# Moving one channel tile of a depthwise convolution from VectorE to GpSimd, and fewer taps at both ends of the GLU projection

## Chip, cores and metric

One NeuronCore of a Trainium2 chip runs the whole kernel. The metric is device time in microseconds, the median of several executions. TensorE does matmuls and transposes, VectorE (DVE in the rows), ScalarE (ACT) and GpSimd (POOL) do elementwise work, and SyncE (SP) issues most of the DMAs.

## What is computed

One layer of a decoder for a prompt of 1024 tokens and 8 sequences of 4 new tokens (1056 tokens together, float32):

```python
z = rms_norm(x) @ w_in        # q, k, v | GLU value, GLU gate | gate a, gate b
u = ua * sigmoid(ub)                            # (T, 1024)
c = conv(u_ext, width 31, one filter per channel) + b   # causal, depthwise
A = three-group dilated window attention @ w_att
B = silu(layer_norm(c)) @ w_conv_out
x = x + (sigmoid(ga) * A + sigmoid(gb) * B) @ w_out
x = x + swiglu(rms_norm(x))
```

The outputs also hold the updated key/value windows and the last 30 rows of `u`. The depthwise convolution of one channel is a sum of 31 products: output token t takes `w[tau] * u[t + tau]` for tau from 0 to 30, from `u` with 30 rows of history ahead of it.

## The kernel before

Activations lie with channels on the 128 partitions: 1024 channels are 8 tiles (`KT`), each 1056 tokens long, handled by TensorE in three chunks of 352 (`NCH`). Every product in full precision is split into three matmuls (lines 678 to 680), from a high and a low part of both operands. A weight job is one 1024×128 slice of a weight: SyncE loads it into `raw`, ScalarE casts the high part `whi` (line 1140 or 1203), VectorE subtracts to make the low part `wlo` (`split_lo`, line 1428), and TensorE runs 72 matmuls. `raw`, `whi` and `wlo` have two buffers each; the weights of job m + 2 are made when job m is over.

The jobs come in this order, written out by hand on each engine: 16 GLU jobs (0 to 15, two for each channel tile j of `u`), 18 jobs for Q, K and V (16 to 33, three groups of six), 16 jobs for the gates, 8 for the convolution's projection, then attention projection, `w_out` and the FFN. From the gate jobs on, engines walk through 72 slots `q`, one chunk of 352 tokens each. Attention blocks, moves of V and K rows (`moves`, slots 1, 13 and 29 and the ones after), LayerNorm (from slot 22) and the samples' attention are hung on those slots.

The convolution runs on VectorE beside all this. `tap(k, tau)` (lines 1466 to 1472) adds one product for 1024 tokens of channel tile k: the first tap of a tile is a `tensor_scalar`, the other 30 are `scalar_tensor_tensor` with `u` and `conv` as the two tensors. 8 × 31 = 248 taps are spread by fixed counts: 13 after each GLU tile, 5 in each Q/K/V job (split 1, 2, 2 over its chunks, between the evacuations `qkv_out`), and 3 in each slot for the 54 that are left. `sample_conv(k)` (lines 1498 to 1508) does the 32 sample tokens of a tile by a product, a reduction and a bias. It runs for tiles 0 to 5 in every third Q/K/V job, ahead of that job's `split_lo`, and for tiles 6 and 7 behind the last tap of each, in slots 7 and 17.

VectorE's `qkv_out` (lines 1512 to 1527) moves a finished Q/K/V chunk out of PSUM and signals `s_zfd`, for which TensorE's job after next waits; for q and k it needs ScalarE's root of the mean square (`rsb`).

In a gate slot VectorE does, in this order: `split_lo` where it is due, `probs_in`, `maxima`, moves, then the slot's taps. `maxima` is followed by ScalarE's exponentials (`pb`, line 1246) and TensorE's transposes of them (`turn_probs`, line 879).

GpSimd issues DMAs only: 16 cache copies from HBM to HBM at fixed points (`cache_copy`, line 625; each waits for a certain `wlo`), then the cache tiles for the samples' attention, which wait for the end of LayerNorm, and more cache copies.

Of the kernel before, what the change touches and what calls it, by code (L numbers as in the profile page):

```python
# [17 lines left out]
F32 = mybir.dt.float32  # L18
F32R = mybir.dt.float32r
ALU = mybir.AluOpType  # L20
# [4 lines left out]
P = 128  # L25
D = 1024
SEQ = 1024
DEC_B, DEC_S = 8, 4
NS = DEC_B * DEC_S
T = SEQ + NS  # L30
NCH = 3
CH = T // NCH
PC2 = SEQ - 2 * CH
KT = D // P
HD = 64
NG, NH = 3, 4
# [4 lines left out]
CW = 31  # L41
HIST = CW - 1
SEG = HIST + DEC_S
ULEN = HIST + SEQ + DEC_B * SEG
# [15 lines left out]
QKV0 = GLU0 + 2 * KT  # L60
# [23 lines left out]
KTILES = [1] * 10 + [1, 2, 1, 2, 1, 2, 1] + [0] + [1] * 4  # L84
KTILE_SLOT = 31

TAPS_GLU = 13
TAPS_QKV = 5
TAPS_SLOT = 3
V_B, V_LW, V_LB, V_NF = CW, CW + 1, CW + 2, CW + 3  # L90
NVEC = CW + 4
# [3 lines left out]
def build(nc, a):  # L95
# [4 lines left out]
    def at(name, shape, dt, offset):  # L100
        return nc.alloc_sbuf_tensor_at(name, shape, dt, offset=offset)
# [16 lines left out]
    vec = perm("vec", [P, KT, NVEC])  # L118
# [14 lines left out]
    conv = at("conv", [P, KT, T], F32, S3)  # L133
# [5 lines left out]
    U0 = misc + 5 * T * 4  # L139
    u = at("u", [P, KT, ULEN], F32, U0)  # L140
# [46 lines left out]
    pb = reg("pb", [P, NH, 2 * P])  # L187
    kvv = reg("kvv", [P, KT, GW])
    assert cur2[0] <= nc.sbuf_usable_end
    rowqk = at("rowqk", [P, NG, 2, HD], F32, U0 + KT * ULEN * 4 + 3 * GW * 4)  # L190
    cur2 = [cur2[0] - KT * GW * 4]
    prow = reg("prow", [P, NG, 2 * P])
# [37 lines left out]
    def sem(name):  # L230
        return ctx.enter_context(nc.semaphore(name))
# [7 lines left out]
    s_hi, s_lo, s_pe = sem("s_hi"), sem("s_lo"), sem("s_pe")  # L239
    s_z = [sem(f"s_z{i}") for i in range(2)]  # L240
    s_zfd = [sem(f"s_zfd{i}") for i in range(2)]
    s_g, s_gfd, s_a, s_af = (sem(n) for n in ("s_g", "s_gfd", "s_a", "s_af"))
    s_ufree = sem("s_ufree")
    s_sig = sem("s_sig")
    s_sq, s_ssr, s_msr, s_sqrt = sem("s_sq"), sem("s_ssr"), sem("s_msr"), sem("s_sqrt")
    s_ztd, s_zta = sem("s_ztd"), sem("s_zta")
    s_zst = [sem(f"s_zst{i}") for i in range(2)]
# [86 lines left out]

        return ob[n % 4] if n < 2 * KT else ob2[(n - 2 * KT) % 3]

    TAP0 = KT * TAPS_GLU + 6 * NG * TAPS_QKV

    UNITS = [("att", c * KT + j) for c in range(2) for j in range(KT)] + [("out", 0), ("out", 1)]
    UNITS += [("att", 2 * KT + j) for j in range(KT)] + [("out", o) for o in range(2, DNG)]  # L340
# [275 lines left out]
    @block.gpsimd  # L616
    def _(pool):
        caches = ("cache_kv_w128", "cache_kv_w512", "cache_kv_w2048")

        def cache_copy(g, b, q=0, parts=1):  # L620
            keep = WIN[g] - DEC_S
            src = a[caches[g]][0, b, DEC_S:WIN[g]].rearrange("t k h d -> t (k h d)")
            dst = a[f"kv_sample{g}"][0, b, 0:keep].rearrange("t k h d -> t (k h d)")
            r = slice(q * keep // parts, (q + 1) * keep // parts)
            pool.dma_start(dst[r, :], src[r, :]).then_inc(s_cache, 16)

        for b in range(DEC_B):
            pool.wait_ge(s_lo, 2 * b + 3)
            cache_copy(0, b)
        for b in range(DEC_B):  # L630
            pool.wait_ge(s_lo, 4 * b + 3)
            cache_copy(1, b)

        def cache_tile(n, kind, g, b):

            c = a[caches[g]][0, b, :, kind].rearrange("t h d -> t (h d)")
            if n >= 3 and n - 3 < NB:

                pool.wait_ge(s_sc, n - 3 + 1)
            elif n >= 3:  # L640

                pool.wait_ge(s_kcf, n - 3 - NB + 1)
            if g == 0:
                pool.dma_start(kc[n % 3][:, DEC_S - 1, :], c).then_inc(s_kc[n % 3], 16)
            else:
                pool.dma_start(kc[n % 3][:, :, :], c.rearrange("(i r) d -> i r d", r=DIL[g])[:, 0:DEC_S, :]).then_inc(s_kc[n % 3], 16)

        pool.wait_ge(s_ln["norm"], NCH)
        for n in range(NB):
            g, b = n // DEC_B, n % DEC_B  # L650
            cache_tile(n, 0, g, b)
            if b == 0:
                pool.wait_ge(s_srows, 16 * (g + 1))
            if n >= 2:

                pool.wait_ge(s_prod, n - 1)
            pool.dma_start(qb[n % 2][:, :, :].rearrange("p s d -> p (s d)"),
                           scr_q[g, 0, DEC_S * b:DEC_S * b + DEC_S, :].rearrange("r d -> (r d)").partition_broadcast(P)).then_inc(s_qb[n % 2], 16)
        for n in range(NB):
            cache_tile(NB + n, 1, n // DEC_B, n % DEC_B)  # L660

        for b in range(DEC_B):
            for q in range(4):
                pool.wait_ge(s_lo, FFN0 + 1 + (4 * b + q) * 2)
                cache_copy(2, b, q, 4)
        pool.dma_start(a["conv_sample"][0, :, 0:HIST - DEC_S, :], a["state_conv"][0, :, DEC_S:HIST, :]).then_inc(s_cache, 16)
# [6 lines left out]
    def _(pe):  # L673
# [163 lines left out]
        def moves(g, part):  # L837
            if part == 0:
                if g == 0:
                    pe.wait_ge(s_urow, 2)  # L840
                    pe.wait_ge(s_zfd[1], NCH * GATE0 // 2)
                elif g == 1:
                    pe.wait_ge(s_Oe, KT)
                else:
                    pe.wait_ge(s_ln["cen"], NCH)
                    pe.wait_ge(s_ln["root"], NCH)
            for i in (range(5) if part == 0 else range(5, NMOVE[g])):
                move(g, i)
# [574 lines left out]
    def _(dve):  # L1423
# [51 lines left out]
        for j in range(KT):  # L1475
            split_lo(0, 2 * j + 2, j + 1)
            for c in range(NCH):
                dve.wait_ge(s_sig, NCH * j + c + 1)
                dve.wait_ge(s_z[0], NCH * j + c + 1)
                n = CH if c < 2 else PC2  # L1480
                last = V.tensor_tensor(u[:, j, HIST + c * CH:HIST + c * CH + n], z(0, c)[:, 0:n], sg[:, c * CH:c * CH + n], ALU.mult)
                if c == 2:
                    last = V.tensor_tensor(u[:, j, HIST + SEQ:].rearrange("p (b r) -> p b r", b=DEC_B)[:, :, HIST:SEG],
                                           z(0, c)[:, n:CH].rearrange("p (b s) -> p b s", b=DEC_B),
                                           sg[:, SEQ:T].rearrange("p (b s) -> p b s", b=DEC_B), ALU.mult)

                last.then_inc(s_zfd[0], 1)
                dve.drain().then_inc(s_zfd[1], 1)
            split_lo(1, 2 * j + 3, j + 1)
            if j == 0:  # L1490
                conv_params()
            for v in range(TAPS_GLU * j, TAPS_GLU * (j + 1)):
                tap(v // CW, v % CW)
        V.tensor_copy(ptail[:, :, :], u[:, :, SEQ:SEQ + HIST])
        V.tensor_copy(utail[:, :, :].rearrange("p k (b s) -> p k b s", b=DEC_B),
# [2 lines left out]
        def sample_conv(j):  # L1498
            us = u[:, j, HIST + SEQ:].rearrange("p (b r) -> p b r", b=DEC_B)
            win = bass.AP(us.tensor, us.offset, [us.ap[0], [SEG, DEC_B], [1, DEC_S], [1, CW]])  # L1500
            wv = vec[:, j, 0:CW]
            wr = bass.AP(wv.tensor, wv.offset, [wv.ap[0], [0, DEC_B], [0, DEC_S], [1, CW]])
            dve.drain()
            V.tensor_tensor(sprod[:, :, :, :], win, wr, ALU.mult)
            dve.drain()
            V.tensor_reduce(conv[:, j, SEQ:T], sprod[:, :, :, :].rearrange("p b s w -> p (b s) w"), AX_X, ALU.add)
            dve.drain()
            return V.tensor_scalar(conv[:, j, SEQ:T], conv[:, j, SEQ:T], vec[:, j, V_B:V_B + 1], None, ALU.add)
# [21 lines left out]
        for g in range(NG):  # L1530
            for i in range(6):
                m = QKV0 + 6 * g + i
                for c in range(NCH):
                    if m > QKV0:
                        qkv_out(m - 1, c)
                    v0 = KT * TAPS_GLU + TAPS_QKV * (m - QKV0)
                    for v in range(v0 + (0, 1, 3)[c], v0 + (1, 3, 5)[c]):
                        tap(v // CW, v % CW)
                if (m - QKV0) % NCH == 0:
                    last = sample_conv((m - QKV0) // NCH)  # L1540
                    if (m - QKV0) // NCH == 4:
                        last.then_inc(s_ufree, 1)
                split_lo(m % 2, m + 2, m // 2 + 1)
# [37 lines left out]
        def ln_sum(c):  # L1581

            if c == 0:
                dve.drain()
            if c == 2:
                dve.wait_ge(s_ln["mean"], 1)
            acc = csum[:, c % 2, :, :]
            V.tensor_tensor(acc, conv[:, 0:2, cols(c)], conv[:, 2:4, cols(c)], ALU.add)
            for k in range(4, KT, 2):
                dve.drain()  # L1590
                V.tensor_tensor(acc, acc, conv[:, k:k + 2, cols(c)], ALU.add)
            dve.drain()
            V.tensor_tensor(acc[:, 0, :], acc[:, 0, :], acc[:, 1, :], ALU.add).then_inc(s_ln["sum"], 1)
# [108 lines left out]
        for q in range(NSLOT):  # L1702
# [11 lines left out]
            for g in range(NG):  # L1714
# [3 lines left out]
                if q == MOVE_SLOT[g] + 1:  # L1718
                    for i in range(5, NMOVE[g], 2):
                        move_rows[0](dve, g, i, s_kvd)  # L1720
            for v in range(TAP0 + TAPS_SLOT * q, min(TAP0 + TAPS_SLOT * (q + 1), KT * CW)):
                tap(v // CW, v % CW)
                if v == (KT - 1) * CW - 1:
                    sample_conv(KT - 2)
                if v == KT * CW - 1:
                    sample_conv(KT - 1)
                    dve.drain()
            if q == MEAN_SLOT - 1:
                ln_sum(0)
                ln_sum(1)  # L1730
# [202 lines left out]
```

## Time and profile before

| | |
|---|---|
| Median of 3 executions | 1866.09 us (1861.48 to 1867.97) |
| The profiled execution | 1861.45 us |
| Its span, first to last instruction | 1859.7 us |
| TensorE, VectorE, ScalarE, GpSimd busy | 95%, 56%, 34%, 4% of the span |
| Mean granted clock of TensorE | 0.968 of full speed |

In a timeline or chain, a row gives start and duration in us, engine and line, and the result and inputs by name. A bracket holds the idle time of the engine just ahead of it and what ended it. `DVEq` is VectorE's instruction queue (drains, semaphores), `PEld` is the weight load.

### The profile page before, as it was taken

The page shows a single profiled execution, that of the slowest core. Times are in us where ns is not written, and L with a number is a line of the kernel's source. Part 1 is how long each engine was busy: PE and PEld are TensorE (multiplying, and loading weights), DVE is VectorE, ACT ScalarE, POOL GpSimd, SP SyncE. Part 2 cuts the span into 40 slices and gives each one's busy share as a digit, 9 for nine tenths or more (in the row PEclk, how much of TensorE's full clock was granted, in tenths as well). Part 3 has the DMA queues.
Part 4 walks back from the last instruction along what each step waited for, and adds up shares of the span by engine and source line. Part 5 has one row for each costly group of instructions (what it writes and reads, how often), then busy time and mean ns, then how long its engine had stood idle before and what let it go on. Part 6 is the DMA issues. An engine that isn't in the chain of part 4 may idle for free.

```text
span 1859.7 us, 25335 instructions
## 1 busy us (share of the span) xinstructions
PE 1764.4 (95%) x10357; PEld 1656.8 (89%) x10357; DVE 1046.0 (56%) x1464; ACT 623.6 (34%) x1029; POOL 69.8 (4%) x125
## 2 busy tenths in 40 slices
PE   6999989999999887689999999999999999999999
PEld 5899989999888877679998889899899899899897
DVE  5688888788887665663275432424424424424425
ACT  5111165957566676710122322111111111111110
POOL 0000000000000011212000000000000000000000
PEclk8999999999999998888799999999999999999999
DMA  6111333234342436965382012222222222222232
GB/s 191 57 56 56 102 112 115 92 114 139 102 141 87 143 114 201 341 220 174 103 277 91 1 37 96 93 90 87 91 93 87 93 90 87 94 90 88 93 109 103
DMA packets 156487, 211.55 MB, mean 114 GB/s; under 512 B 9090, under 2 KB 127010, under 8 KB 155603
## 3 DMA queue, kind: packets, MB, share of 16 engines
q1 hardware_dynamic: 145971, 134.01, 23.4%
q0 software_dynamic: 10416, 76.16, 10.8%
q8 instruction: 68, 1.11, 0.2%
q14 instruction: 32, 0.26, 0.0%
HBM read 180.04 MB, written 74.80 MB: 137 GB/s over the span
## 4 chain that ended last, share of the span: by engine, by line
PE 83%; DVE 7%; DMA 4%; DVEq 2%; SPq 2%; ACT 1%; issue 1%; ACTq 0%
PE ps L678 19%; PE ps L679 19%; PE ps L680 19%; PE ps L1116 4%; PE ps L1114 4%; PE ps L1115 4%; DVE conv L1472 2%; PE ps L945 2%; PE ps L1044 2%; PE ps L1046 2%; PE ps L1045 2%; DMA qb<-scr_q 2%; DMA raw<-w_in 1%; PE ps L892 1%; SPq L474 1%
## 5 line engine op out<-in xcount | busy, mean ns | idle before, releaser
L678 PE MATMUL ps<-xhi,whi 128*128 128x352 f32 x1200 | 406.5, 339 | 8.6 <-DVEq L1527 7.0
L680 PE MATMUL ps<-xhi,wlo 128*128 128x352 f32 x1200 | 389.1, 324 | 0.0
L679 PE MATMUL ps<-xlo,whi 128*128 128x352 f32 x1200 | 388.6, 324 | 0.0
L678 PE MATMUL ps<-nhi,whi 128*128 128x352 f32 x1056 | 341.7, 324 | 0.0
L679 PE MATMUL ps<-nlo,whi 128*128 128x352 f32 x1056 | 339.4, 321 | 0.0
L680 PE MATMUL ps<-nhi,wlo 128*128 128x352 f32 x1056 | 339.0, 321 | 0.0
L1472 DVE SCALAR_TENSOR_TENSOR conv<-u,vec,conv 128x1024 f32<-128x1024 f32 x240 | 308.3, 1284 | 25.6 <-issue 11.1
L1428 DVE TENSOR_TENSOR wlo<-raw,whi 128x1024 fp32r<-128x1024 f32 x126 | 153.5, 1220 | 254.7 <-ACT whi L1203 246.5
L678 PEld LDWEIGHTS ps<-xhi,whi 128*128 128x128 f32 x1200 | 228.9, 191 | 19.6 <-DVEq L1527 7.6
L679 PEld LDWEIGHTS ps<-xlo,whi 128*128 128x128 f32 x1200 | 229.2, 191 | 4.4 <-issue 0.2
L680 PEld LDWEIGHTS ps<-xhi,wlo 128*128 128x128 f32 x1200 | 228.4, 190 | 0.0
L678 PEld LDWEIGHTS ps<-nhi,whi 128*128 128x128 f32 x1056 | 198.9, 188 | 1.1
L679 PEld LDWEIGHTS ps<-nlo,whi 128*128 128x128 f32 x1056 | 199.1, 189 | 0.4
L680 PEld LDWEIGHTS ps<-nhi,wlo 128*128 128x128 f32 x1056 | 198.6, 188 | 0.0
L1203 ACT CAST whi<-raw 128x1024 fp32r<-128x1024 f32 x90 | 93.9, 1045 | 279.0 <-PE ps L1109 209.2
L1867 DVE TENSOR_TENSOR x<-x,ps 128x512 f32<-128x512 f32 x176 | 118.2, 686 | 78.8 <-PE ps L1116 78.4
L1116 PE MATMUL ps<-whi,aclo 128*128 128x512 f32 x352 | 138.8, 394 | 0.0
L1114 PE MATMUL ps<-whi,achi 128*128 128x512 f32 x352 | 138.8, 394 | 0.0
L1115 PE MATMUL ps<-wlo,achi 128*128 128x512 f32 x352 | 138.2, 393 | 0.0
L1854 DVE TENSOR_TENSOR sil<-ps,sil 128x352 f32<-128x352 f32 x66 | 34.6, 525 | 124.4 <-PE ps L680 124.4
L1404 ACT ACTIVATE sil<-ps 128x352 f32<-128x352 f32 x66 | 30.7, 465 | 190.4 <-PE ps L680 190.4
L678 PE MATMUL ps<-shi,whi 128*128 128x352 f32 x192 | 69.0, 360 | 25.3 <-DVE slo L1696 24.5
(214 smaller groups left out, 2242.8 us busy)
## 6 DMA issues: line engine op xcount, KB each, us to landing
kv_sample<-cache_kv_w POOLq DMA_DIRECT2D x32, 1022.0 KB, 6.4
raw<-w_in SPq DMA_DIRECT2D x50, 512.0 KB, 4.6
raw<-w_gate_up SPq DMA_DIRECT2D x44, 512.0 KB, 3.9
scr_z<-zt SPq DMA_DIRECT2D x34, 528.0 KB, 3.2
kc<-cache_kv_w POOLq DMA_DIRECT2D x32, 512.0 KB, 6.1
qb<-scr_q POOLq DMA_DIRECT2D x24, 512.0 KB, 6.5
raw<-w_down SPq DMA_DIRECT2D x22, 512.0 KB, 4.2
kv_sample<-cache_kv_w POOLq DMA_DIRECT2D x8, 1016.0 KB, 6.5
```

Source lines behind the costliest of these rows:

```text
L678: pe_mm(out, wh, rhs_hi, start=first, stop=False)
L679: pe_mm(out, wh, rhs_lo, start=False, stop=False)
L680: return pe_mm(out, wl, rhs_hi, start=False, stop=last)
L945: mm = nc.tensor.matmul(ps[:, 3, hp * P + col:hp * P + col + w], kc[m % 3][:, s if g else DEC_S - 1, hp * P:(hp + 1) * P], ptr[:, g, 0, co ...
L1044: nc.tensor.matmul(dst, hhi[:, k, tok], wohi[half][:, k, :], start=k == 0, stop=False)
L1114: nc.tensor.matmul(dst, achi[i % 2][:, k, tok], whi[half][:, cc], start=k == 0, stop=False)
L1115: nc.tensor.matmul(dst, achi[i % 2][:, k, tok], wlo[half][:, cc], start=False, stop=False)
L1116: mm = nc.tensor.matmul(dst, aclo[i % 2][:, k, tok], whi[half][:, cc], start=False, stop=k == 1)
L1203: act.copy(whi[n % 2][:, :], raw[n % 2][:, :]).then_inc(s_hi, 1)
L1428: V.tensor_tensor(wlo[slot][:, :], raw[slot][:, :], whi[slot][:, :].bitcast(F32), ALU.subtract).then_inc(s_lo, 1)
L1472: return V.scalar_tensor_tensor(dst, src, w, dst, ALU.mult, ALU.add)
L1867: last = V.tensor_tensor(x1_half(t, half), x1_half(t, half), ps[0:n, d % RING, :], ALU.add)
```

## The change

The 31 taps of channel tile 7 go to GpSimd. It starts when the last GLU tile of `u` is there (`s_zfd[0]`), multiplies each shifted row into one of two new buffers `ctap`, drains, and adds that to `conv`: one `tensor_scalar` for tap 0, then 30 times a `tensor_scalar` and a `tensor_tensor`. It signals `s_conv` behind the last. Four of the 1016 KB cache copies now stand ahead of this on GpSimd's queue and four behind it. `ctap` lies over the start of buffers that the attention stage uses, so TensorE waits for `s_conv` before the first `moves`, and VectorE waits for it before the first sum of LayerNorm.

VectorE keeps 217 taps. It runs 6 after the first GLU tile and 8 after the last (13 before), 3 in the first Q/K/V job (5 before), and three in each of slots 0 to 12. The sample convolutions of tiles 6 and 7 stand in slots 2 and 4.

```diff
--- before.py
+++ after.py
@@ -84,8 +84,9 @@
 KTILES = [1] * 10 + [1, 2, 1, 2, 1, 2, 1] + [0] + [1] * 4
 KTILE_SLOT = 31
 
-TAPS_GLU = 13
-TAPS_QKV = 5
+TAPS_GLU = (6, 13, 13, 13, 13, 13, 13, 8)
+TAPS_QKV = (3, 5)
+KT_DVE = KT - 1
 TAPS_SLOT = 3
 V_B, V_LW, V_LB, V_NF = CW, CW + 1, CW + 2, CW + 3
 NVEC = CW + 4
@@ -187,6 +188,7 @@
     pb = reg("pb", [P, NH, 2 * P])
     kvv = reg("kvv", [P, KT, GW])
     assert cur2[0] <= nc.sbuf_usable_end
+    ctap = [at(f"ctap{i}", [P, SEQ], F32, U0 + KT * ULEN * 4 + 2048 + i * SEQ * 4) for i in range(2)]
     rowqk = at("rowqk", [P, NG, 2, HD], F32, U0 + KT * ULEN * 4 + 3 * GW * 4)
     cur2 = [cur2[0] - KT * GW * 4]
     prow = reg("prow", [P, NG, 2 * P])
@@ -241,7 +243,7 @@
     s_zfd = [sem(f"s_zfd{i}") for i in range(2)]
     s_g, s_gfd, s_a, s_af = (sem(n) for n in ("s_g", "s_gfd", "s_a", "s_af"))
     s_ufree = sem("s_ufree")
-    s_sig = sem("s_sig")
+    s_sig, s_conv = sem("s_sig"), sem("s_conv")
     s_sq, s_ssr, s_msr, s_sqrt = sem("s_sq"), sem("s_ssr"), sem("s_msr"), sem("s_sqrt")
     s_ztd, s_zta = sem("s_ztd"), sem("s_zta")
     s_zst = [sem(f"s_zst{i}") for i in range(2)]
@@ -334,7 +336,7 @@
 
         return ob[n % 4] if n < 2 * KT else ob2[(n - 2 * KT) % 3]
 
-    TAP0 = KT * TAPS_GLU + 6 * NG * TAPS_QKV
+    TAPQ = [sum(TAPS_GLU) + (TAPS_QKV[0] + (n - 1) * TAPS_QKV[1] if n else 0) for n in range(6 * NG + 1)]
 
     UNITS = [("att", c * KT + j) for c in range(2) for j in range(KT)] + [("out", 0), ("out", 1)]
     UNITS += [("att", 2 * KT + j) for j in range(KT)] + [("out", o) for o in range(2, DNG)]
@@ -627,7 +629,22 @@
         for b in range(DEC_B):
             pool.wait_ge(s_lo, 2 * b + 3)
             cache_copy(0, b)
-        for b in range(DEC_B):
+        for b in range(4):
+            pool.wait_ge(s_lo, 4 * b + 3)
+            cache_copy(1, b)
+
+        pool.wait_ge(s_zfd[0], NCH * KT)
+        for tau in range(CW):
+            k = KT - 1
+            dst, src, w = conv[:, k, 0:SEQ], u[:, k, tau:tau + SEQ], vec[:, k, tau:tau + 1]
+            if tau == 0:
+                last = nc.gpsimd.tensor_scalar(dst, src, w, vec[:, k, V_B:V_B + 1], ALU.mult, ALU.add)
+            else:
+                nc.gpsimd.tensor_scalar(ctap[tau % 2][:, :], src, w, None, ALU.mult)
+                pool.drain()
+                last = nc.gpsimd.tensor_tensor(dst, dst, ctap[tau % 2][:, :], ALU.add)
+        last.then_inc(s_conv, 1)
+        for b in range(4, DEC_B):
             pool.wait_ge(s_lo, 4 * b + 3)
             cache_copy(1, b)
 
@@ -837,6 +854,7 @@
         def moves(g, part):
             if part == 0:
                 if g == 0:
+                    pe.wait_ge(s_conv, 1)
                     pe.wait_ge(s_urow, 2)
                     pe.wait_ge(s_zfd[1], NCH * GATE0 // 2)
                 elif g == 1:
@@ -1489,7 +1507,7 @@
             split_lo(1, 2 * j + 3, j + 1)
             if j == 0:
                 conv_params()
-            for v in range(TAPS_GLU * j, TAPS_GLU * (j + 1)):
+            for v in range(sum(TAPS_GLU[:j]), sum(TAPS_GLU[:j + 1])):
                 tap(v // CW, v % CW)
         V.tensor_copy(ptail[:, :, :], u[:, :, SEQ:SEQ + HIST])
         V.tensor_copy(utail[:, :, :].rearrange("p k (b s) -> p k b s", b=DEC_B),
@@ -1533,8 +1551,8 @@
                 for c in range(NCH):
                     if m > QKV0:
                         qkv_out(m - 1, c)
-                    v0 = KT * TAPS_GLU + TAPS_QKV * (m - QKV0)
-                    for v in range(v0 + (0, 1, 3)[c], v0 + (1, 3, 5)[c]):
+                    v0, n = TAPQ[m - QKV0], TAPQ[m - QKV0 + 1] - TAPQ[m - QKV0]
+                    for v in range(v0 + n * c // NCH, v0 + n * (c + 1) // NCH):
                         tap(v // CW, v % CW)
                 if (m - QKV0) % NCH == 0:
                     last = sample_conv((m - QKV0) // NCH)
@@ -1581,6 +1599,7 @@
         def ln_sum(c):
 
             if c == 0:
+                dve.wait_ge(s_conv, 1)
                 dve.drain()
             if c == 2:
                 dve.wait_ge(s_ln["mean"], 1)
@@ -1718,13 +1737,12 @@
                 if q == MOVE_SLOT[g] + 1:
                     for i in range(5, NMOVE[g], 2):
                         move_rows[0](dve, g, i, s_kvd)
-            for v in range(TAP0 + TAPS_SLOT * q, min(TAP0 + TAPS_SLOT * (q + 1), KT * CW)):
+            for v in range(TAPQ[-1] + TAPS_SLOT * q, min(TAPQ[-1] + TAPS_SLOT * (q + 1), KT_DVE * CW)):
                 tap(v // CW, v % CW)
-                if v == (KT - 1) * CW - 1:
-                    sample_conv(KT - 2)
-                if v == KT * CW - 1:
-                    sample_conv(KT - 1)
-                    dve.drain()
+            if q in (2, 4):
+                sample_conv(KT - 2 + (q - 2) // 2)
+            if q == 4:
+                dve.drain()
             if q == MEAN_SLOT - 1:
                 ln_sum(0)
                 ln_sum(1)
```

## Rows read from the trace of the kernel before

**Rows 1.** The page: busy time by engine, and TensorE and VectorE in 40 slices.

```profile
PE 1764.4 (95%) x10357; PEld 1656.8 (89%) x10357; DVE 1046.0 (56%) x1464; ACT 623.6 (34%) x1029; POOL 69.8 (4%) x125
...
PE   6999989999999887689999999999999999999999
...
DVE  5688888788887665663275432424424424424425
```

**Rows 2.** Busy time of each engine in four windows, then TensorE's granted clock.

```profile
core 0: us, PE busy (x) PEld busy (x) DVE busy (x) ACT busy (x) POOL busy (x), PEclk, DMA share, GB/s
60.00:85.00 25.00, 24.81 (x145) 23.91 (x144) 20.36 (x21) 1.98 (x3) 0.49 (x1) 0.90 0.14 43
262.00:440.00 178.00, 178.00 (x1068) 171.82 (x1067) 144.28 (x148) 132.03 (x164) 1.46 (x3) 1.00 0.33 101
225.50:456.00 230.50, 223.49 (x1330) 215.49 (x1329) 192.06 (x193) 160.31 (x197) 2.15 (x5) 0.99 0.39 127
255.70:263.20 7.50, 7.47 (x34) 7.25 (x35) 6.87 (x7) 2.22 (x3) 0.22 (x1) 0.74 0.61 203
```

**Rows 3.** Chain of waits, 225 to 262 us (start, us, what); timeline of ScalarE and TensorE.

```profile
226.82 1.28 DVE conv L1472
...
245.80 1.28 DVE conv L1472
247.16 1.29 DVE conv L1472
...
251.24 1.19 DVE sprod L1504
...
253.92 1.22 DVE wlo L1428
...
258.16 0.29 PE ps L679
...
260.12 0.16 PE ps L678
...
235.87 1.04 ACT L1140 CAST whi<-raw 128x1024 fp32r<-128x1024 f32 x1
...
255.73 0.66 PE L678 MATMUL ps<-xhi,whi 128*128 128x352 f32 x1 [7.01 <-DVEq L1527]
```

**Rows 4.** Timeline of TensorE ahead of `moves` and `turn_probs`.

```profile
471.13 1.94 PE L824 MATMUL ps<-ident,vt 128*128 128x128 f32 x16 [0.89 <-ACT urows L1209]
...
489.12 1.12 PE L879 MATMUL ps<-ident,pb 128*128 128x128 f32 x4 [2.81 <-ACT pb L1246]
...
596.96 1.55 PE L879 MATMUL ps<-ident,pb 128*128 128x128 f32 x8 [2.10 <-ACT pb L1246]
```

**Rows 5.** VectorE: groups by shape and waits, 262 to 440 us; taps; timeline.

```profile
L1472 DVE SCALAR_TENSOR_TENSOR conv<-u,vec,conv 128x1024 f32<-128x1024 f32 x69 | 88.6, 1284 | 9.8 <-issue 7.7
...
L1428 DVE TENSOR_TENSOR wlo<-raw,whi 128x1024 fp32r<-128x1024 f32 x14 | 17.0, 1218 | 0.0
...
L1504 DVE TENSOR_TENSOR sprod<-u,vec 128x992 f32<-128x992 f32 x4 | 4.8, 1193 | 0.3
...
DVE zt L1523 <- ACT rsb L1194: 22.8, 24, 2.2
...
L1472 DVE SCALAR_TENSOR_TENSOR conv<-u,vec,conv x240: 1283/1284/1290, 64.1 to 587.4; 128x1024 f32<-128x1024 f32 x120
...
L1471 DVE TENSOR_SCALAR conv<-u,vec x8: 811/812/814, 63.2 to 523.3; 128x1024 f32<-128x1024 f32 x8
...
64.05 16.24 DVE L1472 SCALAR_TENSOR_TENSOR conv<-u,vec,conv 128x1024 f32<-128x1024 f32 x12
...
306.55 1.28 DVE L1472 SCALAR_TENSOR_TENSOR conv<-u,vec,conv 128x1024 f32<-128x1024 f32 x1 [0.18 <-issue]
```

**Rows 6.** Timeline of GpSimd; DMA issues (KB each, median us to landing).

```profile
306.22 0.49 POOL L625 DMA_DIRECT2D kv_sample<-cache_kv_w  x1 [50.30 <-DVE wlo L1428]
...
kv_sample<-cache_kv_w POOLq DMA_DIRECT2D x8, 1016.0 KB, 6.5
```

## The prediction

> **What bounds the kernel now.** I read the page first [rows 1]. TensorE is busy 95% of the span and its slices are nines except the first, the sixth (an eight) and the 14th to 18th (605 to 837 us); VectorE stands at seven or eight tenths in most slices up to the 15th and at two to five later. So VectorE's work matters only where TensorE stops for it, and from 837 us on nothing in the diff reaches it. The windows by stage come next [rows 2]: from 262 to 440 us, inside the Q/K/V projection, TensorE is busy 178.00 of 178.00 us, and VectorE 144.28. The reader is to see a stage with no TensorE gap, beside a VectorE with little to spare. The whole projection, 225.5 to 456 us, has 230.5 − 223.49 = 7.0 us of TensorE gap, and the timeline puts all of it at one place, 255.73 us, behind VectorE [rows 3]. Its chain runs without a hole: from 226.82 us on 13 taps of the last GLU tile, 5 taps and the sample convolution of the first Q/K/V job, and only then the `wlo` of job 18 [rows 3]. ScalarE's `whi` for that job had been there since 235.87 + 1.04 = 236.9 us, so VectorE alone was late. Last I read the slots after 470 us, where VectorE's chain passes through `maxima` and ScalarE's exponentials back to TensorE: waits of 2.81 us at 489.12 and 2.10 us at 596.96 [rows 4].
>
> **What is removed from VectorE.** 31 of 248 taps go. The median tap takes 1.284 us and the next follows 1.36 us after it [rows 3, 5]. They leave at three places.
> - First tile, 13 to 6 taps: 7 × 1.36 = 9.5 us sooner. They lie between 64 and 80 us, where TensorE is busy 24.81 of 25 us [rows 2, 5], under its own matmuls of the second tile: worth nothing in time.
> - Last tile 13 to 8, first Q/K/V job 5 to 3: 7 taps, 9.5 us, out of the chain that makes the 7.0 us gap. `wlo` of job 18 would end at 253.92 + 1.22 − 9.5 = 245.6 us, behind its `whi` and 3 us before TensorE stopped (255.73 − 7.01 = 248.7). Without the gap: 7.0 us. Behind the gap the matmuls step 0.29 us instead of 0.16 until 259.62, some 13 of them: TensorE's granted clock had gone to 1.2 GHz after it stood still, and returned to 2.4 [rows 2, 3]. 13 × 0.13 = 1.7 us go too.
> - 17 taps in slots 13 to 17 (three a slot, the last at 587 us): 23 us of VectorE. Only the wait of 2.10 us behind them is exposed, with 0.5 us that I put on slower matmuls after it [rows 4]: 2.6 us.
>
> **What is moved on VectorE.** The sample convolutions of tiles 6 and 7 (253.92 − 251.24 = 2.7 us for one [rows 3]) go from slots 7 and 17 to slots 2 and 4. In slot 2 one stands right ahead of `wlo` and the first `maxima` on VectorE, the chain that already makes TensorE wait 2.81 us: +2.7 us. The one in slot 4 goes with the second taken out of slot 17: zero, since TensorE's next wait at a `turn_probs` after 489.12 us comes at 596.96 [rows 4].
>
> So with GpSimd left out: −7.0 − 1.7 − 2.6 + 2.7 = **−8.6 us**.
>
> **What is added on GpSimd.** 31 one-input passes and 30 two-input passes of 128×1024 float32, starting when the last GLU tile is written (225.5 us). The trace of before has no arithmetic on GpSimd, only 125 short instructions, 69.8 us in all, nearly all of them DMA issues such as the 0.49 us at 306.22 [rows 1, 6]. Its prices are bounded from rows. Below: GpSimd is no faster than VectorE, 0.812 for one input and 1.218 for two [rows 5], 61.7 us in all, 1.01 a pass. My value: one input as ScalarE's cast of this size, 1.04 [rows 3], and two inputs as twice that, if they come through one reader: 31 × 1.04 + 30 × 2.08 = 95 us, 1.57 a pass. Above: 2.3 a pass, one and a half times my value, 140 us. The Trainium skill, "GPSIMD Engine Reference", Performance versus the Vector engine, gives 4497 ns for a two-input add of 2048 float32; an estimate from that is 2.25 us for each add here, and no row shows it.
>
> By itself that hides. TensorE waits for GpSimd only at its `moves` of group 0, 471.13 us [rows 4]: 245 us for 61 passes, so they would have to take 4.0 us each before it showed. The second new wait, `ln_sum` at 623 us, is later still. Queued behind the convolution on GpSimd are four cache copies of 1016 KB that went out one per 50 us; nothing waits for them before the end.
>
> **The collision.** The question is whether VectorE and GpSimd can both stream from SBUF. From 262 to 440 us VectorE runs 69 taps, 14 `wlo` and 4 `sprod` with two SBUF tensors each: 87 instructions, 110.4 us [rows 5]. With 14 `wlo`, one for each job, and a little over, I take the stretch as 14.1 jobs of 12.6 us: 6.2 such instructions a job, 7.8 us; everything else, gaps included, 3.2 us; waits for ScalarE 22.8/14.1 = 1.6 us [rows 5]. I forecast that such an instruction and a GpSimd pass exclude one another and alternate: each of VectorE's 6.2 waits for one pass. That is not in the trace, and it is what I choose. Added per job: 6.2 × 1.57 = 9.7 us. GpSimd gets 6.2 passes done in it and 3.2/1.57 = 2.0 more beside the rest, 8.2; it needs 61/8.2 = 7.4 jobs. VectorE is then 7.4 × 9.7 = 72 us later. Against that stand the waits for ScalarE that it fills, 7.4 × 1.6 = 12; the 7 taps that left this stretch, 9.5; and its lead, about 4 us: reckoning TensorE's jobs from 255.73 by their matmuls, each `wlo` ends 2 to 6 us before it is needed (my estimate). What is late next is `wlo` of the job after next and the bank that `qkv_out` frees, so TensorE stands: 72 − 12 − 9.5 − 4 = +46 us. This already holds the gap's share, and the later slots give −2.6 + 2.7 ≈ 0. The profiled execution took 1861.45 us (span 1859.7 and 1.75 around it), which gives **1907**. The median of the runs is 4.6 above that execution; I leave it in the range.
>
> By lower prices: 6.2 + 3.2/1.01 = 9.4 passes a job, 6.5 jobs, 6.5 × 6.2 × 1.01 = 41, less 10.4, 9.5 and 4: +17, 1878. By upper: 7.6 a job, 8.0 jobs, 114, less 12.8, 9.5 and 4: +88, 1949. Its own range is 1878 to 1949.
>
> The rows are silent on the exclusion. The Trainium skill, "SBUF — State Buffer", Who interferes with whom, states it: an instruction of VectorE with two SBUF inputs and a GpSimd instruction that reads SBUF lock each other out for the whole instruction, whichever starts first. By that rule the sum is the one above; without it −8.6.
>
> **Rivals.**
> - *They don't disturb each other.* For it: GpSimd's issues fell among taps, the one at 306.22 us right ahead of and into the tap at 306.55, and all 240 taps took 1283 to 1290 ns [rows 5, 6], though an issue is not a pass that reads 4 KB a partition. Then −8.6: 1853, faster. It decides as soon as a pass costs VectorE less than (9.5 + 12 + 4) us over the 46 instructions that it meets, 0.55 us each. Chance 0.24.
> - *They share.* Each slows the other by half a pass: 36 − 12 − 9.5 − 4 = +10.5, 1872. For it: reads are short and could interleave. Chance 0.12. Its mild end is a wash, within 0.3%: 0.08 on its own.
> - *GpSimd always loses.* It starts a pass only beside VectorE's 3.2 us a job and 1.6 of waits, about 3 passes a job: 18 jobs do 54, and the last seven hold up `moves` and everything behind it on TensorE, 7 × 1.57 = 11 us, with VectorE blocked once per pass by what is left of it, some 0.8 us: 61 × 0.8 = 49, less 25.5. About +30, 1892; in the forecast's side, 0.08.
> - *The cache copies bunch.* Four of them at once when the convolution ends, 6.5 us each to land, before one `raw` load [rows 6]: 26 us of queue against 12.6 of a job, at most +15 us. It adds to a case rather than making one; 0.03 more for slower.
>
> **How the numbers follow.** Exclusion 0.45, the other slower cases 0.23, together 0.68; a wash 0.08; faster 0.24. A measurement of this kernel tells 0.3% (5.6 us) from no change. The range must leave out at most 2 in 10, so it reaches to the undisturbed case: 1850 to 1949.
>
> **What would show it.** Right: taps between 226 and 380 us with a mean of 2.3 us or more instead of 1.28 (or gaps as long between them), TensorE waiting for `wlo` or for `qkv_out` in nearly every job there, and its granted clock falling with it. GpSimd's passes should stand at about 1.0 and 2.1 us. Undisturbed: taps at 1.28, no gap at 255, GpSimd done by 330. Sharing: taps near 2. Wrong by size: if a two-input pass takes 3 us the loss passes 90 us, and a last pass after the first slots would show a wait of TensorE ahead of `moves`.

## The result, and the profile after

The changed kernel takes 1891.96 us in the median of 4 executions (1891.49 to 1894.32), the kernel before 1863.93 us in the 4 taken beside it: ratio 1.0152, 95% interval 1.0135 to 1.0169. It is slower by 28 us. The forecast was slower, 1907 us, with a range of 1850 to 1949; the direction and the place are right, the rise over the profiled execution was forecast as 46 us and is 30.4 (1891.81 against 1861.45).

The changed kernel's page, busy time and slices, against [rows 1]:

```profile
PE 1776.8 (94%) x10357; PEld 1664.0 (88%) x10357; DVE 1061.2 (56%) x1433; ACT 623.7 (33%) x1029; POOL 266.5 (14%) x186
...
PE   6999998889899977959999999999999999999999
...
DVE  5489899997984464664247342424424424424425
...
POOL 0000189993000001221100000000000000000000
```

VectorE has 31 instructions less and is busy 15 us longer. It is fullest in the slices in which GpSimd works. The window of the Q/K/V projection, as in [rows 2], shows 24.3 us without a matmul where there were 7.0, and the waits of TensorE from 225 to 520 us name one cause (us in total, times, longest):

```profile
225.50:456.00 230.50, 206.21 (x1183) 195.61 (x1182) 215.45 (x165) 135.28 (x168) 199.26 (x67) 0.97 0.32 103
```

```profile
PE ps L695 <- DVEq L1545: 26.8, 13, 3.5
```

Line 1545 is where `qkv_out` tells TensorE that a bank is free (1527 before). The single wait of 7.01 us [rows 3] has become 13 waits of up to 3.5 us. The projection ends late, and nothing is lost after it: `moves` starts here, as before in [rows 4] at 471.13:

```profile
L841 PE MATMUL ps<-ident,vt x48: 272/273/421, 500.6 to 704.9; 128*128 128x128 f32 x48
```

500.6 − 471.1 = 29.5 us of the 30.4. Busy time from the start of the projection to the first `moves`, before and then after:

```profile
225.50:471.10 245.60, 237.73 (x1423) 229.13 (x1421) 205.93 (x208) 165.31 (x203) 2.15 (x5) 0.99 0.39 126
```

```profile
225.50:500.60 275.10, 248.16 (x1428) 235.24 (x1426) 251.10 (x204) 165.78 (x204) 199.26 (x67) 0.97 0.35 112
```

So the 29.5 us have two parts: TensorE stands still for 26.9 us instead of 7.9, and it is busy for 10.4 us more with the same matmuls, at a lower mean granted clock (0.97 instead of 0.99). VectorE by shape, 226 to 450 us, and its longest tap over the whole run, against [rows 5]; then GpSimd by shape:

```profile
L1490 DVE SCALAR_TENSOR_TENSOR conv<-u,vec,conv 128x1024 f32<-128x1024 f32 x76 | 138.8, 1826 | 11.1 <-issue 8.3
L1446 DVE TENSOR_TENSOR wlo<-raw,whi 128x1024 fp32r<-128x1024 f32 x15 | 24.8, 1651 | 0.3 <-ACT whi L1158 0.3
L1541 DVE SCALAR_TENSOR_TENSOR zt<-ps,qkw,rsb 128x352 f32<-128x352 f32 x24 | 17.0, 706 | 0.0
L1522 DVE TENSOR_TENSOR sprod<-u,vec 128x992 f32<-128x992 f32 x5 | 8.0, 1600 | 0.4
...
L1524 DVE TENSOR_REDUCE conv<-sprod 128x32 f32<-128x992 f32 x5 | 5.9, 1186 | 0.4
L1489 DVE TENSOR_SCALAR conv<-u,vec 128x1024 f32<-128x1024 f32 x3 | 5.0, 1661 | 0.3 <-issue 0.2
L1526 DVE TENSOR_SCALAR conv<-conv,vec 128x32 f32<-128x32 f32 x5 | 4.1, 822 | 0.4
```

```profile
L1490 DVE SCALAR_TENSOR_TENSOR conv<-u,vec,conv x210: 1283/1285/3299, 64.4 to 584.6; 128x1024 f32<-128x1024 f32 x105
```

```profile
L643 POOL TENSOR_SCALAR ctap<-u,vec 128x1024 f32<-128x1024 f32 x30 | 113.4, 3779 | 0.0
L645 POOL TENSOR_TENSOR conv<-conv,ctap 128x1024 f32<-128x1024 f32 x30 | 82.8, 2758 | 15.8 <-issue 11.7
```

Taps went from 1284 to 1826 ns, `wlo` from 1218 to 1651, `sprod` from 1193 to 1600 [rows 5]. What reads one SBUF tensor and a PSUM bank (`zt`, line 1541) or reduces one tensor (line 1524) kept its duration. The `zt` rows also show 0.0 us of waiting for ScalarE, where the stretch before had 22.8 [rows 5]. That is how to read a stretched instruction: the sum of busy time grows, and an idle time elsewhere on the same engine shrinks.

The timelines of both engines laid side by side, GpSimd first, show the mechanism: VectorE's instructions with two SBUF inputs wait for an addition to end, and GpSimd waits for them.

```profile
254.65 3.39 POOL L645 TENSOR_TENSOR conv<-conv,ctap 128x1024 f32<-128x1024 f32 x1
258.02 3.83 POOL L643 TENSOR_SCALAR ctap<-u,vec 128x1024 f32<-128x1024 f32 x1
261.99 2.82 POOL L645 TENSOR_TENSOR conv<-conv,ctap 128x1024 f32<-128x1024 f32 x1
```

```profile
254.53 4.61 DVE L1490 SCALAR_TENSOR_TENSOR conv<-u,vec,conv 128x1024 f32<-128x1024 f32 x2 [0.18 <-issue]
259.06 0.57 DVE L1541 SCALAR_TENSOR_TENSOR zt<-ps,qkw,rsb 128x352 f32<-128x352 f32 x1
259.81 2.74 DVE L1490 SCALAR_TENSOR_TENSOR conv<-u,vec,conv 128x1024 f32<-128x1024 f32 x2 [0.18 <-issue]
262.46 3.43 DVE L1446 TENSOR_TENSOR wlo<-raw,whi 128x1024 fp32r<-128x1024 f32 x1
```

The addition of 261.99 ends at 264.81; the `wlo` that was issued at 262.46 ends at 265.89, 1.08 us later, which is nearly its full 1.22 us: it did next to nothing until the addition was over. The second tap of the pair from 254.53 ends at 259.14, 1.10 us after the addition of 254.65 ended (258.04). The two taps at 259.81 run inside the record of the multiplication of 258.02 and take 2.74 us, where two undisturbed ones take 2.64: a multiplication does not shut them out as an addition does.

### The profile page after: what moved, and what is told of

It reads as the page before. It is cut to its first block, busy times and chain, and to the rows that moved or that the text cites. A ratio compares the mean times of both kernels' runs of the same rounds, so it can differ in the third digit from the quotient of the medians.

```text
span 1890.0 us, 25366 instructions
## 1 busy us (share of the span) xinstructions
PE 1776.8 (94%) x10357; PEld 1664.0 (88%) x10357; DVE 1061.2 (56%) x1433; ACT 623.7 (33%) x1029; POOL 266.5 (14%) x186
## 3 DMA queue, kind: packets, MB, share of 16 engines
q0 software_dynamic: 10416, 76.16, 10.7%
## 4 chain that ended last, share of the span: by engine, by line
PE 72%; DVE 11%; DVEq 7%; DMA 4%; issue 2%; ACT 2%; SPq 2%; ACTq 0%
PE ps L695 16%; PE ps L696 16%; PE ps L697 16%; DVEq L1545 6%; DVE conv L1490 5%; PE ps L1134 4%; PE ps L1132 4%; PE ps L1133 4%; PE ps L963 2%; PE ps L1062 2%; PE ps L1064 2%; PE ps L1063 2%; DMA qb<-scr_q 1%; DMA raw<-w_in 1%; PE ps L910 1%
## 5 line engine op out<-in xcount | busy, mean ns | idle before, releaser
L1446 DVE TENSOR_TENSOR wlo<-raw,whi 128x1024 fp32r<-128x1024 f32 x126 | 160.0, 1272 | 272.6 <-ACT whi L1221 255.9
L627 POOL DMA_DIRECT2D kv_sample<-cache_kv_w x48 | 23.6, 493 | 1098.5 <-DVE wlo L1446 1098.5
L643 POOL TENSOR_SCALAR ctap<-u,vec 128x1024 f32<-128x1024 f32 x30 | 113.4, 3779 | 0.0
## 6 DMA issues: line engine op xcount, KB each, us to landing
kv_sample<-cache_kv_w POOLq DMA_DIRECT2D x8, 1016.0 KB, 10.7
```

The costliest lines, as they stand in the source:

```text
L643: nc.gpsimd.tensor_scalar(ctap[tau % 2][:, :], src, w, None, ALU.mult)
L1446: V.tensor_tensor(wlo[slot][:, :], raw[slot][:, :], whi[slot][:, :].bitcast(F32), ALU.subtract).then_inc(s_lo, 1)
```

## The experiments

Ten kernels. In those that leave taps out, channel tile 7 of the result is incomplete. The first four ran on one chip with 23 executions of the kernel before (median 1862.89 us), the next four with 17 (1863.51), the last two with 11 (1861.67). Ratios are against those.

**One pass on GpSimd.** Only tap 0 of channel tile 7; its other 30 taps are left out.

```diff
-        for tau in range(CW):
+        for tau in range(1):
             k = KT - 1
```

> GpSimd runs one pass of the 61 (tap 0 of channel tile 7); the other 30 taps of that tile are left out. Everything else of the change stands: the fewer taps on VectorE, the two waits on s_conv, the order of the cache copies, the moved sample convolutions. Theory (VectorE's instructions with two SBUF inputs and GpSimd's passes exclude each other): taps back at 1.28 us, no TensorE gap near 252 us, and the time is before minus 8.6, about 1855. Rival (the edits around the passes cost the time: the waits, the cache copies that bunch, the sample convolutions in slots 2 and 4): 1880 to 1890, with taps at 1.28 all the same.

Measured: 1854.87 us, ratio 0.995 (0.9933 to 0.9967). Taps from 226 to 450 us are at 1285 ns and the window of [rows 2] has no gap:

```profile
L1490 DVE SCALAR_TENSOR_TENSOR conv<-u,vec,conv 128x1024 f32<-128x1024 f32 x88 | 113.1, 1285 | 12.9 <-issue 9.8
```

So all that the change does besides the passes is a gain of 0.5%, as summed (−8.6 us), and the whole loss, 1891.96 − 1854.87 = 37 us, belongs to 60 passes. The new waits cost nothing that shows, and the moved sample convolution is seen in slot 2, where TensorE's wait for the exponentials is 5.07 us instead of the 2.81 of [rows 4]:

```profile
482.99 0.90 PE L897 MATMUL ps<-ident,pb 128*128 128x128 f32 x3 [5.07 <-ACT pb L1264]
```

The four cache copies cannot be judged here, since without the passes they don't bunch.

**Multiplications alone.** 31 one-input passes; the 30 additions are left out.

```diff
-                nc.gpsimd.tensor_scalar(ctap[tau % 2][:, :], src, w, None, ALU.mult)
+                last = nc.gpsimd.tensor_scalar(ctap[tau % 2][:, :], src, w, None, ALU.mult)
                 pool.drain()
-                last = nc.gpsimd.tensor_tensor(dst, dst, ctap[tau % 2][:, :], ALU.add)
```

> GpSimd runs the 31 one-input passes (tap 0 and 30 multiplications into ctap), each followed by the drain; the 30 additions are left out. Theory, exclusion for the whole pass: a pass alone takes 1.19 us, VectorE is held up at most 31 x 1.19 = 37 us in all, of which the waits for ScalarE (23 us in the stage) and the 9.5 us of removed taps absorb nearly all: 1855 to 1865, and taps beside the passes show stretches of up to 1.2 us. Rival, any two streams slow each other in proportion to bytes: a one-input pass moves two thirds of a two-input pass, so this run carries 40% of the 28 us and of the stretch: about 1866.

Measured: 1857.03 us, ratio 0.9968 (0.9953 to 0.9984). GpSimd's group, then VectorE's taps and `wlo` from 226 to 450 us:

```profile
L643 POOL TENSOR_SCALAR ctap<-u,vec 128x1024 f32<-128x1024 f32 x30 | 102.0, 3399 | 15.9 <-issue 15.9
```

```profile
L1489 DVE SCALAR_TENSOR_TENSOR conv<-u,vec,conv 128x1024 f32<-128x1024 f32 x88 | 119.9, 1363 | 12.9 <-issue 9.8
L1445 DVE TENSOR_TENSOR wlo<-raw,whi 128x1024 fp32r<-128x1024 f32 x17 | 22.9, 1345 | 0.3 <-ACT whi L1157 0.3
```

A multiplication is recorded with 3.4 us in the mean and yet takes only about 0.4 us from VectorE: 88 × 0.078 for the taps, 17 × 0.127 for `wlo` and 2.6 us in three smaller groups are 11.7 us over 30 passes. Single rows, GpSimd first, say why:

```profile
263.95 2.85 POOL L643 TENSOR_SCALAR ctap<-u,vec 128x1024 f32<-128x1024 f32 x1 [0.16 <-issue]
```

```profile
264.18 1.97 DVE L1489 SCALAR_TENSOR_TENSOR conv<-u,vec,conv 128x1024 f32<-128x1024 f32 x1 [0.19 <-issue]
```

The tap ends at 266.15. With its own 1.28 us it began to run at 264.87, 0.9 us after the multiplication started, and it was over 0.65 us before the multiplication's record ended. Eight such rows of this run put that start at 0.91 to 0.97 us. The multiplication's record is 2.85 us long, no longer than with nothing beside it (the run without taps, below). So a multiplication shuts a tap out for about its first 0.9 us only; in the rest of its record taps run beside it. Only what exceeds 2.85 us in a record is GpSimd waiting.

**Additions alone.** Tap 0 and 30 two-input passes over `u`; the multiplications and tile 7's sum are left out.

```diff
-                nc.gpsimd.tensor_scalar(ctap[tau % 2][:, :], src, w, None, ALU.mult)
+                last = nc.gpsimd.tensor_tensor(ctap[tau % 2][:, :], u[:, k, 0:SEQ], src, ALU.add)
                 pool.drain()
-                last = nc.gpsimd.tensor_tensor(dst, dst, ctap[tau % 2][:, :], ALU.add)
```

> GpSimd runs tap 0 and 30 two-input passes (an addition of two shifted rows of u into ctap), each followed by the drain; the multiplications and the sum of channel tile 7 are left out. Theory, exclusion for the whole pass: VectorE is held up by up to 30 x 2.7 = 81 us where it has a two-input instruction ready, twice as much as by the multiplications: 1870 to 1885. Rival, a fixed price for each pass whatever it reads (55 us of stretch over 61 passes, 0.9 us each): the same as with the multiplications alone, within 3 us.

Measured: 1888.35 us, ratio 1.0127 (1.0094 to 1.016), a little past the upper end of what was expected.

```profile
L643 POOL TENSOR_TENSOR ctap<-u 128x1024 f32<-128x1024 f32 x30 | 87.0, 2901 | 16.6 <-issue 12.6
```

```profile
L1489 DVE SCALAR_TENSOR_TENSOR conv<-u,vec,conv 128x1024 f32<-128x1024 f32 x75 | 125.8, 1677 | 11.1 <-issue 8.4
L1445 DVE TENSOR_TENSOR wlo<-raw,whi 128x1024 fp32r<-128x1024 f32 x15 | 27.0, 1797 | 0.3 <-ACT whi L1157 0.3
```

75 × 0.392 + 15 × 0.579 and 5.8 us in the smaller groups are 43.9 us over 30 additions: 1.46 us each. A fixed price for a pass is ruled out. Above the run with one pass, the two halves add 2 and 33 us, and both together 37.

**Writes alone.** Tap 0 and 60 memsets of the same size; the other 30 taps are left out.

```diff
-                nc.gpsimd.tensor_scalar(ctap[tau % 2][:, :], src, w, None, ALU.mult)
+                nc.gpsimd.memset(ctap[0][:, :], 0.0)
                 pool.drain()
-                last = nc.gpsimd.tensor_tensor(dst, dst, ctap[tau % 2][:, :], ALU.add)
+                last = nc.gpsimd.memset(ctap[1][:, :], 0.0)
+                pool.drain()
```

> GpSimd runs tap 0 and 60 passes that only write (a memset of 128x1024 float32 into ctap), each followed by a drain; the other 30 taps of channel tile 7 are left out. Theory (what VectorE and GpSimd exclude each other over is the reading of SBUF): the taps stay at 1.28 us and the time is that of the run with one pass, about 1855. Rival (any GpSimd instruction that touches SBUF, or its dispatch, holds VectorE up): taps are stretched by some 0.3 us or more in the stage and the time is above 1865. One-input VectorE instructions in the wide mode (the bias of the sample convolution, tap 0 of a tile) may be stretched under either.

Measured: 1853.5 us, ratio 0.995 (0.9935 to 0.9965). GpSimd's two groups, and the taps:

```profile
L645 POOL MEMSET ctap<- 128x1024 f32 x30 | 29.1, 971 | 16.6 <-issue 13.2
L643 POOL MEMSET ctap<- 128x1024 f32 x30 | 28.7, 956 | 3.4
```

```profile
L1491 DVE SCALAR_TENSOR_TENSOR conv<-u,vec,conv 128x1024 f32<-128x1024 f32 x89 | 114.3, 1285 | 13.1 <-issue 10.0
```

60 passes that write 4 KB a partition leave the taps where they were. So neither GpSimd's writing nor its being busy costs the taps anything. What is left is its reading; no run here reads without also computing.

**No taps of VectorE in the Q/K/V jobs** but for the first of a tile; the others of those 88 are left out.

```diff
-                        tap(v // CW, v % CW)
+                        if v % CW == 0:
+                            tap(v // CW, v % CW)
```

> The changed kernel with VectorE's taps in the Q/K/V jobs left out but for the first tap of a tile, so that GpSimd's 61 passes run with little beside them. Theory (a pass as recorded holds waiting for VectorE, most of all in the multiplications): the multiplications fall from 3.78 us to about 1.2 us and the additions from 2.76 to about 2.3, and GpSimd is done some 120 us after it starts instead of 213. Rival (the passes are slow by themselves): 3.8 and 2.8 stay.

Measured once: 1850.36 us. GpSimd's last pass ends at 414.0 us instead of 438.8, not at about 350 as expected. Both expectations fell in part. The addition goes to 2.38 us, as the theory said; the multiplication has 2.85 us of its own and not 1.2 (GpSimd first, VectorE behind it):

```profile
290.70 2.84 POOL L643 TENSOR_SCALAR ctap<-u,vec 128x1024 f32<-128x1024 f32 x1
293.68 2.39 POOL L645 TENSOR_TENSOR conv<-conv,ctap 128x1024 f32<-128x1024 f32 x1
296.05 3.82 POOL L643 TENSOR_SCALAR ctap<-u,vec 128x1024 f32<-128x1024 f32 x1
```

```profile
293.79 3.36 DVE L1446 TENSOR_TENSOR wlo<-raw,whi 128x1024 fp32r<-128x1024 f32 x1 [0.36 <-ACT whi L1158]
```

Here a single collision stands alone: VectorE's `wlo` arrives while the addition runs. The addition starts at 293.68, `wlo` is issued at 293.79 and ends at 297.15, 1.08 us after the addition's end at 296.07; the multiplication that GpSimd issues next is 0.98 us longer than the undisturbed one, the time `wlo` then needed. Each waits until the other is over. And although the passes ran in full here and the four cache copies bunched behind them, no loss is left, so the copies are not likely to be what made the changed kernel slow.

**Half of the pairs.** Taps 0 to 15 on GpSimd, the other 15 left out.

```diff
-        for tau in range(CW):
+        for tau in range(16):
             k = KT - 1
```

> GpSimd computes taps 0 to 15 of channel tile 7 and leaves out the other 15: half of its pairs. Theory (a pair of passes costs VectorE 1.85 us, 1.47 for the addition and 0.38 for the multiplication, and VectorE's waits for ScalarE in the stretch absorb some): 15 x 1.85 = 28 us of stretch over about 7 jobs, of which about 10 us are absorbed: 16 to 20 us above the run with one pass, about 1872. Rival (the loss comes from one place, as the first collision or a late end, and not from each pass): near 1855 or near 1890.

Measured: 1870.95 us, ratio 1.0039 (1.0025 to 1.0054), 16 us above the run with one pass and 21 below all 30 pairs. The loss grows with the pairs. Whether it grows faster in the second half is within the spread of the runs; VectorE's waits for ScalarE, which absorb part of it, fell to 10.9 us in this run and to none with all pairs.

**The multiplication in two steps.** Tap 0, then 30 passes that multiply and add the bias, as tap 0 does; the additions are left out.

```diff
-                nc.gpsimd.tensor_scalar(ctap[tau % 2][:, :], src, w, None, ALU.mult)
+                last = nc.gpsimd.tensor_scalar(ctap[tau % 2][:, :], src, w, vec[:, k, V_B:V_B + 1], ALU.mult, ALU.add)
                 pool.drain()
-                last = nc.gpsimd.tensor_tensor(dst, dst, ctap[tau % 2][:, :], ALU.add)
```

> GpSimd runs tap 0 and then 30 passes of the same form as tap 0 (multiply, then add the bias, into ctap), each followed by the drain; the 30 additions into channel tile 7 are left out. It asks why the recorded multiplication takes 2.85 us undisturbed where tap 0 took 1.20. If the form matters (one step or two), the passes take about 1.2 us; if the position does (tap 0 is followed by another pass at once, the others by a drain), they take 2.8 us or more as the multiplications did, and VectorE's taps stay within 0.1 us of 1.28 as there.

Measured once: 1858.29 us. The form matters, and the other way round than one would guess: with more work per element the pass is shorter, 2.00 us in the mean with VectorE beside it, against 3.40 in one step, and its shortest rows are at 1.2 us.

```profile
L643 POOL TENSOR_SCALAR ctap<-u,vec 128x1024 f32<-128x1024 f32 x30 | 60.0, 2000 | 16.8 <-issue 16.8
```

```profile
L1489 DVE SCALAR_TENSOR_TENSOR conv<-u,vec,conv 128x1024 f32<-128x1024 f32 x87 | 121.4, 1395 | 12.8 <-issue 9.8
```

VectorE's taps lose 0.11 us each, just over the 0.1 us expected. All its stretched groups together lose 14.8 us over the 30 passes, 0.5 us each, against 0.4 for the slow form: the pass is shorter, but its price to VectorE is not lower. Why the one-step form is slow stays open.

**All taps on VectorE, fewer at the end of the GLU projection.** Three versions, GpSimd as before. The edit is the tuples, written here in short; `tap` is driven by them as in the changed kernel.

```diff
-TAPS_GLU = 13
-TAPS_QKV = 5
+TAPS_GLU = (14,) * 7 + (8,)              # 54 taps left for the slots
+TAPS_GLU = (14,) + (15,) * 6 + (10,)     # or these: 46 left
+TAPS_GLU = (13,) * 7 + (8,)              # or these: 61 left
+TAPS_QKV = (3, 5)
```

> All 248 taps on VectorE and nothing on GpSimd but DMAs, as before; only the counts are changed: 14 taps after each of the first seven GLU tiles and 8 after the last, 3 in the first Q/K/V job, so that the same 54 are left for the slots. Theory (all that the changed kernel gained came from the shorter chain at the start of the Q/K/V projection): the 7.0 us wait of TensorE at 255.73 us and the 1.7 us of slow matmuls behind it go, 8.7 us or 0.5% faster than before, about 1855. Rival (that gain needs a VectorE with 31 taps less, since the taps that leave the ends fill the GLU jobs, which have some 2 us free in 24): TensorE waits in the GLU jobs instead, and the time is within 3 us of before.

Measured: 1858.0 us, ratio 0.9974 (0.9963 to 0.9985). Between the two expectations: the gap at 255 us is gone, but the GLU jobs run some 3 us longer and TensorE waits there, if only for 1.0 us in sum.

```profile
PE ps L679 <- DVE u L1482: 1.0, 3, 0.5
```

> All 248 taps on VectorE, with more of them in the GLU jobs: 14, six times 15, 10 after the last, 3 in the first Q/K/V job, so that 46 instead of 54 are left for the slots. Theory: the GLU jobs have some 2 us of VectorE free in 24, so two more taps (2.7 us) in each of six pairs run 0.7 us over, which its lead covers at first; five taps less in the chain at the end take 6.8 of the 7.0 us; the waits near 590 us shrink by up to 2 us: 1853 to 1857. Rival (VectorE falls behind in the GLU jobs): TensorE waits there from the fourth tile on and the time is that of before or above.

Measured: 1870.59 us, ratio 1.0036 (1.0023 to 1.0049). The rival was right: VectorE is overfull in the GLU jobs, and the wait for `u` from 60 to 230 us grows.

```profile
PE ps L679 <- DVE u L1482: 7.6, 5, 1.9
```

> All 248 taps on VectorE. Only the end of the GLU projection is changed: 8 taps after the last GLU tile, 3 in the first Q/K/V job, 13 after each other GLU tile as before; the 7 taps go to the slots, three each in slots 0 to 20. Theory: the wait of TensorE at the start of the Q/K/V projection (7.0 us and 1.7 us of slow matmuls) goes and nothing is given back in the GLU jobs, where the version with 14 taps gave back some 4 us: about 1855, the time of the run with one pass. Rival: the slots 18 to 20, which had no taps, give it back through the exponentials, within 3 us of before.

Measured: 1852.73 us, ratio 0.995 (0.9931 to 0.9968). The window of [rows 2] is full:

```profile
225.50:456.00 230.50, 230.50 (x1391) 222.60 (x1390) 192.17 (x195) 162.20 (x199) 1.94 (x4) 1.00 0.40 129
```

This is the version that beats both kernels, with the full computation and by counts alone: 0.5% below before, 2% below the changed one. It is as fast as the changed kernel without its passes, though VectorE runs 31 taps more.

## Why the prediction was right, and where its sizes were off

**Taken off VectorE, without GpSimd: −8.6 us.** Right. The run with one pass has 0.995 ± 0.0017, that is −9.3 ± 3.2 us. The 7.0 us gap and the slow matmuls behind it carry it: the version with nothing but those seven taps moved has the same ratio. The 9.5 us out of the first GLU tile were put at nothing, and the traces bear it out: the last tile of `u` is finished at 225.9 us in the changed kernel and at 225.2 before. In the slots the sample convolution was priced at +2.7 us, and the wait of 2.81 us became one of 5.07: +2.3. The 17 taps were priced at −2.6, and the wait of 2.10 us ahead of 596.96 is gone in the changed kernel. (Two of the 17 stood in slot 12 and not behind it, which changes nothing.)

**GpSimd by itself hides.** Right. It was done at 438.8 us, `moves` started at 500.6, and the bunched copies (10.7 us to land instead of 6.5 [rows 6]) held nobody that a view names. Its prices were too low for all that: undisturbed 2.85 us for a multiplication and 2.38 for an addition, where 1.04 and 2.08 were put in (the estimate of 2.25 beside them was nearer for the addition). Over the 61 passes 1.04 and 2.08 give a mean of 1.55 and not 1.57, a slip worth 1 us.

**The collision: +46 us.** Right in mechanism, and the term that was mis-sized is "added per job: 6.2 × 1.57 = 9.7 us", each two-input instruction of VectorE waiting for one pass, 72 us in all. The measured stretch from 226 to 450 us is 76 × 0.542 for the taps, 15 × 0.433 for `wlo`, 5 × 0.407 for `sprod`, and 3 × 0.849 and 5 × 0.580 for the one-input instructions of lines 1489 and 1526, together 55 us. It was 72 us by forecast and 55 by measurement, and that it is so near is partly luck, since two errors in it pull apart:
- The price of a pass to VectorE. 1.57 was taken for either sort, as an average of 1.04 and 2.08. Measured apart it is 0.4 for a multiplication and 1.46 for an addition, 1.85 for a pair against 3.1. A multiplication lasts longest on GpSimd's record and disturbs least.
- The number of jobs over which it spreads. 7.4 were forecast, since GpSimd was to win a turn for each of VectorE's. It was engaged for 213 us: 61 passes at 3.24 us, one pause of 11.6 us, and 4 us between passes. That is some 15 jobs, most of the projection.

That second error also moves the next term. VectorE's waits for ScalarE absorbed 12 us in the sum; over the longer stretch all of them went, 20 us in the run with one pass and none after. So 55 − 20 = 35 us against 72 − 12 = 60, and between the run with one pass and the changed kernel 37 us were measured. VectorE's lead, 4 us in the sum, would leave 31; it was not measured apart.

The sum left out that the one-input instructions of lines 1489 and 1526 suffer too: 5.4 of the 55 us. It also put slower matmuls at nothing, though it had named the fall of the clock as a sign. TensorE was busy for 10.4 us more up to the first `moves`, a third of the loss (the two windows in the section on the result). The mean granted clock accounts for about 6 of these by an estimate from those windows, 0.03 × 275.1 − 0.01 × 245.6; what made the rest was not told apart.

Its signs would have misled. It wanted taps of 2.3 us or more for exclusion and near 2 for sharing; 1.83 was measured, and the mechanism was exclusion all the same. The mean depends on how many taps meet an addition, so only the timeline tells the two apart.

**The rule behind it.** Whichever starts second waits: the tap of 254.53 was ahead of the addition of 254.65, which took 3.39 us instead of 2.38, and the next tap then waited for that addition. The Trainium skill, "SBUF — State Buffer", Who interferes with whom, has this lock as first come, first served, only against GpSimd instructions that read SBUF, and not for a VectorE instruction with a single SBUF input outside its two-port modes. The traces agree on these counts: `wlo` ends 1.08 us after the addition that preceded it; the memsets cost nothing; `zt` and the reduction kept their durations; lines 1489 and 1526 were stretched. The Trainium skill, "SBUF — State Buffer", Who interferes with whom, also has the lock last for the whole instruction. For additions it did. For the one-step multiplication it did not, and the measurement decides: taps ran inside its 2.85 us from 0.9 us on. That set much of the size here.

**The rivals.** No disturbance is out (taps at 1826 ns). Equal sharing at half a pass is out as a mechanism, since the collision at 293.68 is a whole wait; by its price (36 us against 55) it lay no further off than the forecast. GpSimd always losing was given 1892 us, the measured time, but by chance: it had GpSimd's last seven passes hold up `moves`, and GpSimd was done 62 us before them (and its own terms, 49 − 25.5 + 11, make 34 and not 30). It is out for additions, which VectorE waited for. A multiplication did lose to the instruction that had waited through the addition: 28 of 30 were recorded with 3.8 or 3.9 us, 1 us above the undisturbed ones.

## What to carry to other kernels

Before work goes from VectorE to GpSimd, count VectorE's instructions with two SBUF inputs beside it: here a tap taken off VectorE saved 1.36 us and cost it 1.85, so the move lost even before TensorE was asked. If GpSimd must work beside such instructions, writes (nothing) and one-input passes (0.4 to 0.5 us) were the cheap ones here. And when a change is made of an offload and a rebalancing, run the rebalancing alone: here it was the whole gain and needed no second engine.

## What was not expected of the hardware

- A one-step multiplication of 128×1024 float32 on GpSimd takes 2.85 us undisturbed, while the two-step form has rows of 1.2. A two-input addition takes 2.38.
- The one-step multiplication keeps a tap of VectorE waiting for only the first 0.9 us of its 2.85.
- In every run with more than one pass, GpSimd stood idle once for 11 to 13 us behind its second arithmetic instruction, at about 230 us, whatever came next (11.55 us in the changed kernel, 13.2 in the run with memsets). VectorE ran undisturbed in it. No run tells its cause.
- VectorE's `tensor_scalar` of 32 elements, 0.24 us alone, took 0.82 us in the mean beside GpSimd: a wait for a pass does not shrink with the instruction that waits.
